# Slots of an expert dealt out four partitions apart in a mixture-of-experts encoder step

## The reference

```
gprob = softmax(h @ w_rg + b_rg);  gp, gi = top_k(gprob, 1)         # one of 4 groups
ev, ei = top_k(elog[group gi], 2);  ew = softmax(ev) * gp           # two of its 8 experts
combine[token, group, expert] = ew for the two chosen, else 0
out = sum over the 32 experts e of
      ((silu(h @ w_eg[e]) * (h @ w_eu[e])) * combine[:, e]) @ w_ed[e]   # 1024 -> 512 -> 1024
h = LN2(alpha * h + out + (p @ w_ple_proj) * sigmoid(h @ w_ple_gate))
```

## Time and profile before

| | |
|---|---|
| median of 3 runs | 921.92 us (920.5 to 921.98) |
| profiled execution | 920.81 us, of which the span is 918.3 us |
| PE busy / DVE / ACT / POOL | 859.0 / 383.2 / 294.6 / 76.1 us |
| moved by DMA | 284.87 MB, 310 GB/s in the mean |
| expert weights | 192 DMAs of 1024 KB |
| stores of expert rows | 30, from 451.2 to 869.9 us |

### The profile page before, as it was taken

One profiled execution on the slowest core, in us unless ns is written; L12 is line 12 of the kernel. 1 busy time (PEld: TensorE's weight loads), 2 busy tenths in 40 slices (PEclk: granted clock), 3 DMA queues, 4 the chain that ended last, 5 costly groups with the idle time before them and its releaser, 6 DMA issues.

```text
span 918.3 us, 15455 instructions
## 1 busy us (share of the span) xinstructions
PE 859.0 (94%) x6336; PEld 536.0 (58%) x6336; DVE 383.2 (42%) x720; ACT 294.6 (32%) x333; POOL 76.1 (8%) x82
## 2 busy tenths in 40 slices
PE   7999998999999899899999999998999899989875
PEld 5998777789998797654444434443444353434321
DVE  7599998897675265761111110101010131010127
ACT  3332234666547833243132222212222222111110
POOL 1100000011110000323010000000000000000000
PEclk9999998999999999889999999999999999999997
DMA  9744437659997747818999999999999999999971
GB/s 344 263 156 132 166 117 214 176 155 254 216 269 228 183 182 321 367 46 293 420 418 420 421 421 421 420 420 423 422 419 422 423 421 420 421 420 421 421 273 57
DMA packets 42786, 284.87 MB, mean 310 GB/s; under 512 B 6602, under 2 KB 6858, under 8 KB 9456
## 3 DMA queue, kind: packets, MB, share of 16 engines
q1 hardware_dynamic: 35888, 254.25, 69.4%
q0 software_dynamic: 6560, 27.82, 12.7%
q10 hardware_dynamic: 288, 2.10, 0.5%
HBM read 258.51 MB, written 13.13 MB: 296 GB/s over the span
## 4 chain that ended last, share of the span: by engine, by line
PE 51%; DMA 28%; DVE 4%; ACT 2%; issue 2%; SPq 1%; ACTq 0%; POOLq 0%; DVEq 0%
DMA raw_x<-wstream 25%; PE ps L1560 13%; PE ps L1289 5%; PE ps L1291 5%; PE ps L1290 5%; PE ps L1580 4%; PE ps L1507 4%; PE ps L1537 3%; PE ps L1321 2%; DMA y_tok<-y_sb,dest 1%; DMA y_second<-y_tok 1%; PE ps L1322 1%; PE ps L1323 1%; PE ps L1316 1%; PE ps L1331 1%
## 5 line engine op out<-in xcount | busy, mean ns | idle before, releaser
L1560 PE MATMUL ps<-raw_x,xs 128*64 128x512 f32 x1024 | 233.8, 598 | 24.1 <-DMA raw_x<-wstream 24.1
L1560 PEld LDWEIGHTS ps<-raw_x,xs 128*64 128x64 f32 x1024 | 71.0, 136 | 140.1 <-issue 137.7
L909 DVE SCALAR_TENSOR_TENSOR cT_sb<-uT_sb,conv_par,cT_sb 128x350 f32<-128x350 f32 x240 | 120.7, 578 | 0.7
L1580 PE MATMUL ps<-raw_x,actT 128*64 128x512 f32 x512 | 115.4, 592 | 0.0
L558 ACT ACTIVATE w_hi<-raw_dense 128x2048 fp32r<-128x2048 f32 x41 | 78.3, 1911 | 75.0 <-PE ps L1316 41.1
L1289 PE MATMUL ps<-hT_hi,w_hi 128*128 128x320 f32 x304 | 96.7, 318 | 0.9 <-issue 0.9
L1290 PE MATMUL ps<-hT_lo,w_hi 128*128 128x320 f32 x304 | 94.7, 312 | 0.0
L1072 DVE TENSOR_TENSOR onehot<-iota_r,rankm 128x192 bf16<-128x192 f32 x33 | 11.8, 357 | 179.2 <-PE ps L1537 179.2
L1537 PEld LDWEIGHTS ps<-onehot,h1b 128*128 128x128 bf16 x2304 | 69.1, 98 | 25.7 <-issue 25.7
L1291 PE MATMUL ps<-hT_hi,w_lo 128*128 128x320 f32 x256 | 79.9, 312 | 0.0
L1580 PEld LDWEIGHTS ps<-raw_x,actT 128*64 128x64 f32 x512 | 36.8, 137 | 72.7 <-issue 71.1
(11 more groups left out here) (274 smaller groups left out, 1082.1 us busy)
## 6 DMA issues: line engine op xcount, KB each, us to landing
raw_x<-wstream SPq DMA_DIRECT2D x192, 1024.0 KB, 23.4
raw_dense<-wstream SPq DMA_DIRECT2D x43, 1024.0 KB, 5.8
w_lo<-raw_dense POOLq DMA_DIRECT2D x11, 1024.0 KB, 8.6
w_lo_third<-raw_dense POOLq DMA_DIRECT2D x6, 1024.0 KB, 9.6
y_tok<-nothing POOLq DMA_DIRECT2D x2, 1280.0 KB, 7.7
ln_gb<-ln POOLq DMA_DIRECT2D x2, 1024.0 KB, 8.1
raw_dense<-wstream ACTq DMA_DIRECT2D x2, 1024.0 KB, 12.7
const<-consts SPq DMA_DIRECT2D x1, 1297.5 KB, 15.1
```

Source lines behind the costliest of these rows:

```text
L909: i = stt(out=cT[:, j, :], in0=src, scalar=w, in1=cT[:, j, :], op0=ALU.mult, op1=ALU.add)
L1560: i = mm(ps[64 * h:64 * h + 64, 1 + odd, :], x, w[h][:, k, :], start=half == 0 and k == 0, stop=half == 1 and k == 3)
L1580: i = mm(ps[64 * h:64 * h + 64, 4 + par, :], a, w[:, f, h, :], start=j == 0 and f == 0, stop=j == 1 and f == 1)
```

## The change

The constant row `iota` no longer holds 0, 1, 2, ... but 0, 16, 32, 48, 1, 17, 33, 49, 2, ...: slot 4g + j stands for rank 16j + g. So the tokens of ranks 0 to 15 stand on partitions 0, 4, 8, ..., 60 (and 64 more), those of ranks 16 to 31 on 1, 5, 9, ... The table `slot_dest` is written and read by rank as before; DVE puts the ranks of `dest_rows` into the new order with four copies of 128 x 64, before PE transposes them.

```
+SPREAD = SLOTS // 16
-    c[:, C_IOTA:C_IOTA + 64] = np.arange(64)
+    c[:, C_IOTA:C_IOTA + 64] = np.arange(64).reshape(SPREAD, 16).T.ravel()
...
+    dest_spread = [a.put(f"dest_spread{i}", [128, 2, SLOTS], F) for i in range(2)]
...
         def dests():
+            dve.wait_ge(ss("dest_in"), 64)
+            for i in range(2):
+                for half in range(2):
+                    V.tensor_copy(dest_spread[i][:, half, :].rearrange("p (g j) -> p j g", j=SPREAD),
+                                  dest_rows[i][:, half, :].rearrange("p (j g) -> p j g", j=SPREAD)).then_inc(ss("dest_moved"), 1)
             dve.wait_ge(ss("dest_psum"), 1)
...
         def dest_transposes():
-            pe.wait_ge(ss("dest_in"), 64)
+            pe.wait_ge(ss("dest_moved"), 4)
             for i in range(2):
-                m = tr(ps[:, 0, 128 * i:128 * i + 128], dest_rows[i][:].rearrange("p h s -> p (h s)"), ident)
+                m = tr(ps[:, 0, 128 * i:128 * i + 128], dest_spread[i][:].rearrange("p h s -> p (h s)"), ident)
```

More of the change, by code:

```diff
@@ L281, in _program @@
         "act_T aT_ready y_ready y_taken y_stored y_free slots_moved pos_ready more_ready "
-        "nowhere_set nowhere_out nothing_set dest_put dest_in dest_psum dest_ready "
+        "nowhere_set nowhere_out nothing_set dest_put dest_in dest_moved dest_psum dest_ready "
         "last_set last_psum last_ready y_kept acc_ready sum_psum final_rows y_out "
```

## The result

The changed kernel took 917.12 us (median of 16 runs, 911.2 to 918.62), the kernel before 920.46 us in the runs of the same comparison (16 runs, 917.01 to 923.39). The ratio is 0.9948 with a 95% interval of 0.9932 to 0.9964, so 4.8 us are gained, between 3.3 and 6.3 (the two medians alone lie 3.3 us apart, the two means 4.6). The forecast was 2.9 us. The earlier median of 921.92 us for the kernel before came from three runs; in these sixteen it is 920.46 us. The profiled execution took 916.44 us with a span of 914.3 us, 4.4 us and 4.0 us less than that of before.

What follows compares the result with a forecast made beforehand. The prediction took the 16 DMA engines in the experts' stage as the bound. Its terms, 0 (copies) + 0 (packets) - 2.9 us (lag), brought the median of 921.92 us to 919.0 us, range 917.0 to 921.4 us.

Steps and rivals of the forecast that it cites:

- The bound: Experts' stage: the DMA engines set the time at 418 to 423 GB/s; PE and DVE work is off the path.
- The cause of the lag: Stores' rows on few slots put one engine behind the mean of sixteen, growing 2.4 to 4.6 us over 21 stores.
- the assumed block of four: Stores: slots 0 to 3 taken as one engine's share, four rows costing 0.31 us, 0.11 us above level.
- The base: Whole kernel: the median of 921.92 us from which the forecast gain was subtracted.
- The term of the lag: Experts' weight stream: level rows gain between 2.2 and 3.6 us, middle 2.9 us.
- The term of the end: Read-back behind the weights: level engines might give a further half microsecond or so, not added.
- more than the lag: Rival: level read-back lets DVE and PE start their end sooner, 1.5 to 2.5 us on top, 917.0 us; chance 0.08.
- The copies: Four DVE copies before PE's transposes: 1.0 to 1.7 us, covered by 2.0 us of PE's `down`, so nothing.
- The packets: Stores: number of packets and bytes stays, priced at nothing; at most 0.9 us, kept in the range.
- That rows are not the cause: Rival: lag from an engine slow by itself or otherwise loaded, no change, 921.9 us; chance 0.17 with gains too small.
- that an idle engine is slow by itself: Rival: an engine carrying few rows is slow and now gets the level share, 0 to 3.0 us lost; chance 0.06.

Runs made afterwards that it cites:

- heaped: Changed kernel with another slot order: the first eight ranks all on slots 0 to 3 and 32 to 35; 923.84 us, ratio 1.0045 to the kernel before.
- low_half: Changed kernel with ranks 0 to 31 dealt over slots 0 to 31 only; 917.64 us, ratio 0.9969 to the kernel before.
- twice_before: Kernel before with every store of an expert's rows issued twice, the second time to a table nothing reads; 931.85 us, ratio 1.0138.
- copies_only: Changed kernel's four copies and PE's wait for them, but slots in the order of the kernel before; 919.91 us, ratio 0.9992.
- the five with level dealing: Profiles of three executions of the changed kernel, of low_half and of turned; ratios to the kernel before from 0.9947 to 0.9969.
- late_read_before: Kernel before, with SP waiting for the last 12 chunks of weights before it issues the read-back of y_tok; 922.9 us, ratio 1.0031.
- late_read_after: Changed kernel, with SP waiting for the last 12 chunks of weights before it issues the read-back of y_tok; 919.0 us, ratio 0.9993.
- turned: Changed kernel with the ranks of every second expert starting at 4 in place of 0; 916.86 us, ratio 0.9958 to the kernel before.

## Why the prediction was right in kind and low in size

**The bound.** Right. DMA work in the experts' stage is on the path: heaped rows cost 4.1 us, doubled rows 12.7 us, no rows save 6.2 us, all against the kernel before, while PE's busy time stays (859.0 and 860.8 us) and its waits change.

**The cause of the lag.** Right: rows of few slots loading few engines. It was read from one agreement, 0.107 us of growth per store against 0.11 us worked out, and heaped, low_half and the doubled stores now show it: from expert 10 to expert 31 the lag grew from 3.9 to 10.0 us in heaped and from 3.7 to 8.2 us in twice_before, but only from 1.7 to 2.1 us in the changed kernel. The agreement itself was in part luck. In copies_only, with the rows in the order of before, the same sum gives 3.0 and 4.5 us, which is 0.07 us for each store and not 0.107, and the assumed block of four was really four and four, so that large experts load the first engine twice.

**The base.** The forecast time of 919.0 us stood on 921.92 us, a median of three runs; with the 920.46 us of sixteen it would have been 917.6 us. The measured 917.12 us lies inside the range stated, by 0.12 us; with that base this is luck.

**The term of the lag, -2.9 us.** Right in kind, its size not settled: PE's matmul before expert 31 came 2.5 us sooner in the first profile. Averaged over the profiles, which differ by more than 1 us among themselves, it is some 0.3 us up to expert 10 (549.1 in before and copies_only, 548.8 us in the five with level dealing) and 1.2 us in the stretch (321.1 against 319.9 us), together half of what was forecast.

**The term of the end, 0.** This is the step that failed: the read-back behind the stream was priced at nothing, without a reason. The prediction wrote that level engines would end the read-back together, "that could give a further half microsecond or so, which I don't add". The tail became 1.5 us shorter in the profile pair and 1.0 us in the mean of two against five. From PE's matmul before expert 31 to the first sum it is 1.8 us and 1.7 us (19.7 against 18.1); the mean gives 0.7 us back behind the sum. late_read_before and late_read_after show that this part is there only while the read-back and the last weights overlap. It is not the lag paid a second time: in heaped the lag is 10.0 us and the way to the sum is 19.8 us, as with 4.6. What the profile shows in its place is engines that are busy and move 199 GB/s from 884 to 886 us, where the changed kernel's move 320; why is open. With 1.5 us for the end the forecast would have been 4.4 us, inside the measured interval. This was the rival called "more than the lag", 917.0 us, to which I gave a chance of 0.08.

**The copies, 0.** Right, and with more cover than thought: 0.53 us against 1.0 to 1.7 us.

**The packets, 0.** The number of packets stays, those with rows rise by half; low_half, turned and the changed kernel give no sign of a price, but none of them changes the packets alone.

**The rivals.** That rows are not the cause, and that an idle engine is slow by itself, are both refuted: with the level share on every engine the lag fell. The Trainium skill's remark in "DMA: Bandwidth & Descriptors", "Latency and other measured facts", that engines 7 and 15 are usually slower, shows in no run here, though no view names the engine that is last: low_half and the changed kernel deal rows to all engines, and with 2.6 and 2.1 us the lag is no higher than without rows (2.7 us).

**What stays open.** The spans of the profiled executions average 917.9 us for before and copies_only and 915.4 us for the five with level dealing, 2.5 us apart, while the comparisons of times give 4.3 us. Most of the difference is in which executions were profiled. The spans of all executions are on record: in the mean they are 918.0 us for the kernel before (82 of them) and 914.5 us for the kernels with level dealing (57), 3.5 us apart; so the five profiled ones were 1.0 us longer than their kernels usually are. Another 0.3 us lie outside the span (2.4 us before, 2.1 us with level dealing). To which term that one microsecond belongs I can't say. Nor is it parted how much goes with TensorE's clock. The executions of the changed kernel show a granted clock of 0.981 in the mean, those of the kernel before 0.979, and within a kernel the executions with the higher clock are the shorter ones. In the two profiles the clock was 0.50 (1.2 GHz) from 892 to 898 us before and only from 892 to 894 us after (0.84 from 894 to 896 us), behind PE's idle 5.15 and 4.12 us; so a part of it may follow from the sooner read-back.

## What to carry to other kernels

When a stage is bound by DMA and its transfers are split over engines by partition, small transfers on few partitions load few engines, and the whole stream waits for the fullest of them. To find it, compare at a wait for a known transfer what the last engine has still to do with what all together still move. Deal such rows over the partitions so that each set of four and the four 32 further gets its share, and give a transfer that runs beside the end of the stream a term of its own: here it was 1 to 2 us, and it did not grow with the lag.

## What the runs showed of the hardware

- Without any rows the last engine is still 2.7 us behind the mean, and was 2.2 us behind it 21 experts earlier: that lag is not made by rows.
- A full DMA share does not mean the full rate: from 884 to 886 us the kernel before shows a share of 1.05 with 199 GB/s, against 421 GB/s while the engines move weights alone.
- Four strided copies of 128 x 64 from SBUF to SBUF take 0.53 us on DVE, while one copy of 128 x 256 out of PSUM takes 0.43 us.
